# Mixture-of-experts layer on one core: run each expert whole on TensorE, and load the last weights in the order of their use

## The chip, the cores and the metric

One core of one Trainium2 chip runs the whole program. The metric is the device time of one execution in microseconds (us); lower is better. The kernel before takes 1175.49 us, the median of 3 runs (1172.38 to 1176.23).

## The reference, cut to what matters

A decoder layer on 256 tokens of width 1024, in float32: a mixer of three attention groups and a layer norm, then a mixture of 32 experts, of which each token takes 4, and a second layer norm. The change concerns the experts alone:

```
def expert_block(args):
    e, tok, w = args
    xb = xt[tok]
    gu = xb @ w_gu[e] + b_gu[e]
    gate = jnp.minimum(gu[:, :D_EXPERT], SWIGLU_LIMIT)
    up = jnp.clip(gu[:, D_EXPERT:], -SWIGLU_LIMIT, SWIGLU_LIMIT)
    act = gate * jax.nn.sigmoid(SWIGLU_ALPHA * gate) * (up + 1.0)
    y = act @ w_dn[e] + b_dn[e]
    return (y * w[:, None]).astype(h.dtype)
```

Each expert has 1024 x 2048 gate-up weights and 1024 x 1024 down weights, 8.39 MB and 4.19 MB, and all of them are read from HBM once: 403 MB.

## The kernel before, in words

Each engine has its own program, written out by hand, and semaphores between them. The mixer ends at about 180 us; then the router picks the experts, and the experts run, two to a loop pass (`PAIRS` = 16; the loop has 15 passes).

**Slots.** An expert works on 64 token slots; a gather (L1032) is a matmul of x with a 0/1 matrix and serves both experts of a pair, in two halves of the width, into PSUM banks 6 and 4. ScalarE (ACT) copies both to `xg` in SBUF. Where an expert has more than 64 tokens, blocks of 32 more slots run in `extra_blocks` (L1178), whose count is read from SBUF into a register of each engine (`value_load`, a TENSOR_LOAD in the trace).

**PE, per expert.** `gate_up` (L1074): 4 chunks of 16 instructions, and the bias; results in banks 4 and 5. VectorE (DVE) and ACT make the activation (L1621 to L1627, sigmoid at L696). `act_transposes` (L1109) turns it over, ACT copies it to `actT` (L700), `down` (L1098) multiplies in 4 chunks into bank 7, from where ACT and DVE copy it to `ysb` (L712, L1665). Once a pair, `combine` (L1039) adds both experts' rows to the four accumulators in banks 0 to 3, with the weights `CT` that `weight_transposes` made.

**The order on PE** (loop at L1216): gate-up of expert 2i+1, down of 2i, gather, transposes for 2i+1, extra blocks of 2i+1, gate-up of 2i+2, down of 2i+1, transposes for 2i+2 and of the weights, combine, extra blocks of 2i+2. So down of an expert stands behind the gate-up of the next one.

**The weights.** SBUF holds gate-up weights of two experts (`gu_slot`) and down weights of one (`dn_slot`). SyncE (SP) loads them in chunks of 2 MB and 1 MB (`load_gu`, L347, `load_dn`, L352), all in one queue and in a fixed order (loop at L400): gate-up of expert e+2 when gate-up of e (and its extra blocks) has read a chunk (`guc`, `xguc`), then down of e+1 when down of e has (`dn_used`, `xdnc`). While SP waits for one, nothing behind it is issued. Behind the loop the last down is loaded, and then the parameters of the second layer norm (L426).

Of the kernel before, what the change touches and what calls it, by code (L numbers as in the profile page):

```python
# [13 lines left out]
P = 128  # L14
TOKENS = 256
TB = TOKENS // P
# [4 lines left out]
N_EXPERTS = 32  # L21
TOP_K = 4
PAIRS = N_EXPERTS // 2
# [5 lines left out]
GU_CHUNKS = 4  # L29
DN_CHUNKS = 4  # L30
# [26 lines left out]
def hybrid_layer(nc, x, w_in, b_in, pos_k, pos_v, w1_k, w2_k, w1_v, w2_v, g_out, w_out, ln1_g, ln1_b,  # L57
                 router_w, router_b, w_gu, b_gu, w_dn, b_dn, ln2_g, ln2_b, out):
    with ExitStack() as ctx:
# [255 lines left out]
        def _(sp_):  # L315
# [84 lines left out]
            with sp.Fori(0, PAIRS - 1) as i:  # L400
                for par in range(2):

                    count_extra_blocks(2 * i + par)
                    for c in range(GU_CHUNKS):
                        xc = use_by_extra_blocks(c)
                        sp.wait_ge(s["guc"], i * (2 * GU_CHUNKS) + (par * GU_CHUNKS + c + 1))
                        sp.wait_ge(s["xguc"], xc)
                        load_gu(i + 1, par, c)
                    for c in range(DN_CHUNKS):
                        xc = use_by_extra_blocks(c)  # L410
                        sp.wait_ge(s["dn_used"], i * (2 * DN_CHUNKS) + (par * DN_CHUNKS + c + 1))
                        sp.wait_ge(s["xdnc"], xc)
                        load_dn(i + par, 1 - par, c)

            count_extra_blocks(N_EXPERTS - 2)
            for c in range(DN_CHUNKS):
                xc = use_by_extra_blocks(c)
                sp.wait_ge(s["dn_used"], (N_EXPERTS - 2) * DN_CHUNKS + c + 1)
                sp.wait_ge(s["xdnc"], xc)
                load_dn(PAIRS - 1, 1, c)  # L420
# [102 lines left out]
        def _(act):  # L523
# [201 lines left out]
            sigmoid(1)  # L725
# [3 lines left out]
                           ACT.Copy).then_inc(s["ysb_ok"], 1)  # L729
            act_columns(5, 1)  # L730
            combine_weights(1)
            act.wait_ge(s["nx_ok"], 1)
            extra_blocks(0)
            with act.Fori(0, PAIRS - 1) as i:
                sigmoid(2 * i + 2)
                expert_output(0, 2 * i + 1)
                slots_to_sbuf(0, 6, 2 * i + 3)
                slots_to_sbuf(1, 4, 2 * i + 4)
                act_columns(6, 2 * i + 2)
                extra_blocks(2 * i + 1)  # L740
                sigmoid(2 * i + 3)
                expert_output(1, 2 * i + 2)
                act_columns(5, 2 * i + 3)
                combine_weights(i + 2)
                extra_blocks(2 * i + 2)
            sigmoid(N_EXPERTS)
            expert_output(0, N_EXPERTS - 1)
            act_columns(6, N_EXPERTS)
# [5 lines left out]
        def _(pe):  # L754
# [277 lines left out]
            def gather(h, bank):  # L1032
# [733 lines left out]
```

## Time and profile before

| | |
|---|---|
| median of 3 runs | 1175.49 us |
| the profiled execution | 1174.48 us |
| its span | 1172.5 us |
| mean granted TensorE clock | 0.98 |
| PE busy | 1071.5 us (91%) |
| LDWEIGHTS (PEld) busy | 458.4 us (39%) |
| DVE, ACT, POOL busy | 25%, 12%, 2% |
| moved by DMA | 426.32 MB, mean 364 GB/s |
| loads of gate-up weights | 128 of 2048 KB, median 30.4 us from issue to landing |
| loads of down weights | 128 of 1024 KB, median 24.0 us from issue to landing |

The profiled execution's own time is 2 us longer than its span. The page cuts the span in 40 slices of 29.3 us; the windows of the trace do the same for any stretch. Lines of PE are mostly L758, the helper that all matmuls go through, so groups are told apart by their tiles and counts: a gate-up is x64 instructions on `WB,S` 128*64, a down x32 of them, a gather x32 on `S,X`, a combine x8 on 128*128 x 512, and an extra block's gate-up x64 on 128*32.

### The profile page before, as it was taken

How to read it: one execution, taken by the hardware profiler on the slowest of the kernel's cores; microseconds unless marked ns; L12 is line 12 of the kernel's file. 1: busy time of each engine (PE TensorE's matmuls, PEld its weight loads, DVE VectorE, ACT ScalarE, POOL GpSimd, SP SyncE). 2: the span in 40 equal slices, each digit the busy share in tenths (PEclk: the TensorE clock that was granted, in tenths of full speed). 3: DMA queues.
4: the chain of work that ended last, by engine and by line, in shares of the span. 5: the costliest groups of instructions: out<-in, count | busy, mean ns of one | idle time of the engine just before them, and what ended most of it. 6: DMA issues, size and time to landing. Idle time of an engine off the chain costs nothing.

```text
span 1172.5 us, 14722 instructions
## 1 busy us (share of the span) xinstructions
PE 1071.5 (91%) x5364; PEld 458.4 (39%) x5365; DVE 291.3 (25%) x770; ACT 146.0 (12%) x313; POOL 29.2 (2%) x54
## 2 busy tenths in 40 slices
PE   7999897888999999998989889999999999999983
PEld 6778544332334333323233323333344333333321
DVE  2354645121212212121212212122212212121114
ACT  2044501010011110000000100001011000000000
POOL 3000400000000000000000000000000000000000
PEclk9999998998999999999999989999999999999997
DMA  9623439764999999999999998999999999999993
GB/s 311 247 110 72 168 137 386 301 241 191 405 427 425 428 427 425 428 427 425 427 427 425 427 427 338 427 425 427 427 425 427 427 426 426 427 426 426 427 420 134
DMA packets 48980, 426.32 MB, mean 364 GB/s; under 512 B 5034, under 2 KB 8923, under 8 KB 16155
## 3 DMA queue, kind: packets, MB, share of 16 engines
q1 hardware_dynamic: 48378, 425.37, 87.8%
q10 hardware_dynamic: 576, 0.61, 0.2%
q8 instruction: 16, 0.26, 0.1%
q14 instruction: 10, 0.07, 0.0%
HBM read 424.91 MB, written 1.05 MB: 363 GB/s over the span
## 4 chain that ended last, share of the span: by engine, by line
PE 62%; DMA 28%; DVE 4%; SPq 3%; issue 2%; ACT 1%; DVEq 0%
PE PB L758 60%; DMA WB<-in_w_gate_up_dram 24%; DMA WB<-in_w_down_dram 3%; SPq L347 2%; ACT S L660 0%; DVE S L1519 0%; DMA X<-in_x_dram 0%; PE PB L1112 0%; DVE K L1502 0%; DVE S L1730 0%; PE PB L765 0%; DVE S L1485 0%; SPq L356 0%; DVE S L1621 0%; DVE S L1622 0%
## 5 line engine op out<-in xcount | busy, mean ns | idle before, releaser
L758 PE MATMUL PB<-WB,S 128*64 128x512 f32 (+5 forms) x3456 | 761.7, 593 | 50.7 <-DMA WB<-in_w_gate_up_dram 25.1
L758 PEld LDWEIGHTS PB<-WB,S 128*64 128x64 f32 (+2 forms) x3456 | 250.8, 139 | 540.5 <-issue 456.2
L1621 DVE TENSOR_SCALAR S<-PB 128x512 f32<-128x512 f32 (+1 forms) x34 | 35.9, 1056 | 652.1 <-PE PB L758 652.1
L758 PE MATMUL PB<-S 32*64 32x512 f32 (+5 forms) x464 | 108.1, 589 | 4.3 <-ACT S L692 1.4
L696 ACT ACTIVATE S<-S 128x512 f32<-128x512 f32 x32 | 20.2, 630 | 552.2 <-DVE S L1621 552.2
L758 PEld LDWEIGHTS PB<-S,X 128*128 128x128 f32 x512 | 61.2, 199 | 13.3 <-issue 12.2
L758 PE MATMUL PB<-S,X 128*128 128x128 f32 x512 | 64.3, 286 | 1.0 <-DVE S L1563 1.0
L758 PE MATMUL PB<-S,WB 128*128 128x256 f32 (+2 forms) x336 | 62.2, 385 | 0.4 <-ACT S L534 0.4
L758 PEld LDWEIGHTS PB<-S 32*64 32x64 f32 (+5 forms) x464 | 34.9, 149 | 65.5 <-issue 54.1
L758 PEld LDWEIGHTS PB<-S,WB 128*128 128x128 f32 (+1 forms) x336 | 48.3, 175 | 12.2 <-issue 2.1
L758 PE MATMUL PB<-WB 128*32 128x128 f32 (+8 forms) x276 | 46.1, 354 | 4.4 <-DVE WB L1450 2.8
L1665 DVE COPY S<-PB 64x512 f32<-64x512 f32 x32 | 21.8, 683 | 106.8 <-PE PB L758 106.8
L712 ACT ACTIVATE S<-PB 64x512 f32<-64x512 f32 x32 | 19.0, 594 | 176.2 <-PE PB L758 176.2
L1622 DVE TENSOR_SCALAR S<-PB 128x512 f32<-128x512 f32 (+1 forms) x34 | 36.1, 1062 | 0.1
L758 PEld LDWEIGHTS PB<-WB 128*64 128x64 f32 (+2 forms) x276 | 29.5, 152 | 16.5 <-issue 12.2
L512 POOL TENSOR_TENSOR K<-K 128x1 f32<-128x1 f32 x4 | 3.9, 982 | 993.1 <-DVE K L1515 993.1
L660 ACT ACTIVATE S<-PB 128x512 f32<-128x512 f32 x32 | 19.1, 597 | 45.9 <-PE PB L758 45.9
L1624 DVE SCALAR_TENSOR_TENSOR S<-S 128x512 f32<-128x512 f32 (+1 forms) x34 | 23.5, 692 | 1.2
L1627 DVE TENSOR_TENSOR S<-S 128x512 f32<-128x512 f32 (+1 forms) x34 | 23.5, 691 | 1.2
L1112 PE MATMUL PB<-K,S 128*128 128x128 f32 x128 | 20.2, 280 | 2.3 <-DVE S L1627 2.3
L577 ACT ACTIVATE WB<-WB 128x128 f32<-128x128 f32 (+1 forms) x40 | 17.7, 443 | 21.9 <-DVE WB L1377 21.9
L1112 PEld LDWEIGHTS PB<-K,S 128*128 128x128 f32 x128 | 14.2, 141 | 15.6 <-issue 13.0
(208 smaller groups left out, 345.1 us busy)
## 6 DMA issues: line engine op xcount, KB each, us to landing
WB<-in_w_gate_up_dram SPq DMA_DIRECT2D x128, 2048.0 KB, 30.4
WB<-in_w_down_dram SPq DMA_DIRECT2D x128, 1024.0 KB, 24.0
WB<-in_w_in_dram SPq DMA_DIRECT2D x3, 2048.0 KB, 15.4
WB<-in_w_in_dram SPq DMA_DIRECT2D x1, 2144.0 KB, 10.5
WB<-in_w_in_dram SPq DMA_DIRECT2D x2, 1024.0 KB, 10.9
WB<-in_w_out_dram SPq DMA_DIRECT2D x2, 1024.0 KB, 10.2
WB<-in_w_out_dram SPq DMA_DIRECT2D x1, 2048.0 KB, 7.8
WB<-in_w_in_dram SPq DMA_DIRECT2D x1, 1040.0 KB, 13.5
```

The lines of the kernel that those rows point to most:

```text
L347: sp.dma_start(gu_slot[par][:, kk * c:kk * c + kk, :], src[:, c // 2, 2 * (c % 2):2 * (c % 2) + 2, :]).then_inc(s_gul[par][c], 16)
L577: ins = act.activation(l[:, a:b], l[:, a:b], ACT.Exp, bias=nmx[u % 3][:, c:c + 1], accum_out=sm[u % 3][:, c:c + 1])
L660: act.activation(xg[:, 4 * h:4 * h + 4, :].rearrange("p k s -> p (k s)"), PB[bank][:, :], ACT.Copy)\
L696: act.activation(act_sb, gt, ACT.Sigmoid, scale=SWIGLU_ALPHA).then_inc(s["sig"], 1)
L712: act.activation(ysb[64 * e:64 * e + 64, 1, :], PB[7][64:128, :], ACT.Copy).then_inc(s["ysb_ok"], 1)
L758: return mm_(o, l, r, start=start, stop=stop, skip_group_check=True)
L1112: ins = tr(PB[bank][:, P * c:P * c + P], act_sb[:, P * c:P * c + P], ident)
L1621: ts(by_rows(g), in_order(gate), LIMIT, None, ALU.min).then_inc(s[g_ok], 1)
L1622: ts(by_rows(u), in_order(up), LIMIT, -LIMIT, ALU.min, ALU.max).then_inc(s[clip], 1)
L1624: stt(u, u, 1.0, g, ALU.add, ALU.mult).then_inc(s[upg], 1)
L1627: tt(a, u, a, ALU.mult).then_inc(s[done], 1)
L1665: cp(ysb[64 * e:64 * e + 64, 0, :], PB[7][0:64, :]).then_inc(s["ysb_dv"], 1)
```

## The change

On PE an expert now runs whole: gate-up, three quarters of the gather (for the odd experts) or of the combine (for the even ones, for the pair before), transposes, the last quarter, extra blocks, down. All transposes go to bank 5. ACT and DVE copy the outputs of an expert behind its extra blocks, and ACT copies the transposed activation between the two halves of the gather. For the first expert, ACT makes `CT` before the sigmoid and the combine stands ahead of the transposes. An extra block waits for the copies of banks 4 and 6 ahead of its own gather. On SP the loop is a pass shorter; the last pass is written out with the down loads ahead of the gate-up loads.

```
-            with sp.Fori(0, PAIRS - 1) as i:
+            def next_gu(i, par):
+                for c in range(GU_CHUNKS):
+                    xc = use_by_extra_blocks(c)
+                    sp.wait_ge(s["guc"], i * (2 * GU_CHUNKS) + (par * GU_CHUNKS + c + 1))
+                    sp.wait_ge(s["xguc"], xc)
+                    load_gu(i + 1, par, c)
+
+            def next_dn(i, par):
+                for c in range(DN_CHUNKS):
+                    xc = use_by_extra_blocks(c)
+                    sp.wait_ge(s["dn_used"], i * (2 * DN_CHUNKS) + (par * DN_CHUNKS + c + 1))
+                    sp.wait_ge(s["xdnc"], xc)
+                    load_dn(i + par, 1 - par, c)
+
+            with sp.Fori(0, PAIRS - 2) as i:
                 for par in range(2):
                     count_extra_blocks(2 * i + par)
...
+                    next_gu(i, par)
+                    next_dn(i, par)
+
+            for par in range(2):
+                count_extra_blocks(N_EXPERTS - 4 + par)
+                next_dn(PAIRS - 2, par)
+                next_gu(PAIRS - 2, par)
             count_extra_blocks(N_EXPERTS - 2)
...
+            next_dn(PAIRS - 1, 0)
```

ACT (the loop; DVE's copies of the outputs move likewise):

```
             with act.Fori(0, PAIRS - 1) as i:
                 sigmoid(2 * i + 2)
-                expert_output(0, 2 * i + 1)
                 slots_to_sbuf(0, 6, 2 * i + 3)
+                act_columns(5, 2 * i + 2)
                 slots_to_sbuf(1, 4, 2 * i + 4)
-                act_columns(6, 2 * i + 2)
                 extra_blocks(2 * i + 1)
+                expert_output(1, 2 * i + 2)
                 sigmoid(2 * i + 3)
-                expert_output(1, 2 * i + 2)
                 act_columns(5, 2 * i + 3)
                 combine_weights(i + 2)
                 extra_blocks(2 * i + 2)
+                expert_output(0, 2 * i + 3)
```

PE:

```
-            def extra_blocks(e, loaded, t, pb6_copied, copies, outputs_copied):
+            def extra_blocks(e, loaded, t, pb4_pb6_copied, copies, outputs_copied):
...
                     with pe.Fori(0, count):
+                        pe.wait_ge(s[pb4_pb6_copied], copies)
                         extra_gather()
-                        pe.wait_ge(s[pb6_copied], copies)
...
-            act_transposes(5, 1)
-            weight_transposes()
             pe.wait_ge(s["ysb_ok"], 1)
             pe.wait_ge(s["bdn_ld"], 16)
             combine()
+            act_transposes(1)
+            weight_transposes()
             extra_blocks(0, 1, 0, "ct_sb", 1, 0)
+            down(0, 1, 1, first=True)
             with pe.Fori(0, PAIRS - 1) as i:
-                pe.wait_ge(s["actT"], 2 * i + 1)
                 gate_up(1, i + 1, 2 * i + 2)
-                down(0, i + 1, 2 * i + 1)
                 pe.wait_ge(s["ohs"], i + 2)
                 pe.wait_ge(s["ct_sb"], i + 1)
                 gather(0, 6)
                 pe.wait_ge(s["g_ok"], 2 * i + 2)
-                gather(1, 4)
-                pe.wait_ge(s["xg_ok"], 2 * i + 3)
-                act_transposes(6, 2 * i + 2)
+                gather(1, 4, range(2))
+                act_transposes(2 * i + 2)
+                gather(1, 4, range(2, 4))
+                extra_blocks(1, i + 1, 2 * i + 1, "xg_ok", 2 * i + 4, 2 * i + 1)
+                down(1, i + 1, 2 * i + 2)
+
                 pe.wait_ge(s["xg_ok"], 2 * i + 4)
-                extra_blocks(1, i + 1, 2 * i + 1, "actT", 2 * i + 2, 2 * i + 1)
-
                 gate_up(0, i + 2, 2 * i + 3)
-                down(1, i + 1, 2 * i + 2)
-                act_transposes(5, 2 * i + 3)
-                weight_transposes()
                 pe.wait_ge(s["ysb_ok"], 2 * i + 3)
                 pe.wait_ge(s["ysb_dv"], 2 * i + 2)
-                combine()
+                combine(range(3))
+                act_transposes(2 * i + 3)
+                weight_transposes()
+                combine(range(3, 4))
                 extra_blocks(0, i + 2, 2 * i + 2, "ct_sb", i + 2, 2 * i + 2)
+                down(0, i + 2, 2 * i + 3)
```

What stands in a row on PE in the first half of the loop (an odd expert): `WB,S` x32 is a gate-up, x16 a down, `S,X` x16 a gather. Before:

```order
L758 MATMUL PB<-WB,S 64x512 x32
L1079 REGISTER_ALU
L758 MATMUL PB<-S 64x512 x4
L758 MATMUL PB<-WB,S 64x512 x16
L1221 REGISTER_ALU
L758 MATMUL PB<-S,X 128x128 x16
L1226 REGISTER_ALU
L1112 MATMUL PB<-K,S 128x128 x4
L1228 REGISTER_ALU
L1180 ISA
L1180 TENSOR_LOAD nx
```

And of the change, where L766 is the helper of all matmuls and L1123 the transposes:

```order
L766 MATMUL PB<-WB,S 64x512 x32
L1089 ISA
L766 MATMUL PB<-S 64x512 x4
L1232 REGISTER_ALU
L766 MATMUL PB<-S,X 128x128 x12
L1123 MATMUL PB<-K,S 128x128 x4
L766 MATMUL PB<-S,X 128x128 x4
L1191 ISA
L1191 TENSOR_LOAD nx
```

The down between bias and gather is gone; it stands behind the extra block now, and the load of the block count (`nx`) follows the last quarter of the gather. Before, the ISA row ahead of that load holds a wait for the second copy of the gathered rows (`xg_ok`); in the change it holds none.

The first expert on PE, behind its bias, where the row of `S 128x512 x4` is the combine. Before:

```order
L1112 MATMUL PB<-K,S 128x128 x4
L1117 MATMUL PB<-K,S 128x128 x2
L758 MATMUL PB<-S 128x512 x4
L1180 TENSOR_LOAD nx
L1180 ISA x2
```

And of the change:

```order
L766 MATMUL PB<-S 128x512 x4
L1123 MATMUL PB<-K,S 128x128 x4
L1128 MATMUL PB<-K,S 128x128 x2
L1191 TENSOR_LOAD nx
L1191 ISA x2
```

The combine moved ahead of the transposes, and the first down (not shown) stands between the extra block and the loop's entry, no longer behind the gate-up of the loop's first pass.

## Rows read from the trace of the kernel before

**Rows 1.** The page: GB/s in 40 slices of 29.3 us; the chain by engine

```profile
GB/s 311 247 110 72 168 137 386 301 241 191 405 427 425 428 427 425 428 427 425 427 427 425 427 427 338 427 425 427 427 425 427 427 426 426 427 426 426 427 420 134
...
PE 62%; DMA 28%; DVE 4%; SPq 3%; issue 2%; ACT 1%; DVEq 0%
```

**Rows 2.** Windows: us, busy (x count) of PE, PEld, DVE, ACT, POOL, PEclk, DMA share, GB/s

```profile
225.00:226.00 1.00, 1.00 (x8) 0.43 (x6) 0.00 (x0) 0.00 (x0) 0.00 (x0) 1.00 0.50 197
...
225.00:245.00 20.00, 20.00 (x98) 6.57 (x96) 5.29 (x16) 0.63 (x1) 0.00 (x0) 1.00 0.18 60
250.00:260.00 10.00, 7.81 (x78) 2.61 (x82) 0.00 (x0) 1.30 (x4) 0.00 (x0) 1.00 0.68 265
275.00:295.00 20.00, 20.00 (x98) 6.35 (x96) 3.67 (x6) 0.63 (x1) 0.00 (x0) 1.00 0.18 57
705.00:720.00 15.00, 14.93 (x70) 5.20 (x67) 6.12 (x17) 1.82 (x3) 0.00 (x0) 1.00 0.67 247
```

**Rows 3.** Timeline of one pair, PE and DVE: start us, us, engine, line, operation, count

```profile
716.75 0.66 PE L1112 MATMUL PB<-K,S 128*128 128x128 f32 x4
...
717.70 3.67 PE L758 MATMUL PB<-S 128*128 128x512 f32 x8
...
721.30 13.95 PE L758 MATMUL PB<-WB,S 128*64 128x512 f32 x64
...
736.20 7.09 PE L758 MATMUL PB<-WB,S 128*64 128x512 f32 x32
...
739.06 0.69 DVE L1627 TENSOR_TENSOR S<-S 128x512 f32<-128x512 f32 x1
...
743.22 3.84 PE L758 MATMUL PB<-S,X 128*128 128x128 f32 x32
```

**Rows 4.** The chain in that pair: start us, us, what

```profile
747.70 1.14 issue
```

**Rows 5.** Timeline of experts 0 and 1, PE and SP's queue

```profile
215.89 0.66 PE L1112 MATMUL PB<-K,S 128*128 128x128 f32 x4 [2.30 <-DVE S L1627]
...
216.62 5.28 PE L758 MATMUL PB<-S 128*128 128x512 f32 x8
...
223.65 13.95 PE L758 MATMUL PB<-WB,S 128*64 128x512 f32 x64 [1.75 <-issue]
...
238.55 7.09 PE L758 MATMUL PB<-WB,S 128*64 128x512 f32 x32
...
241.19 5.05 SPq L352 DMA_DIRECT2D WB<-in_w_down_dram  x4
...
251.22 1.07 PE L758 MATMUL PB<-X,S 128*32 128x256 f32 x16 [1.38 <-issue]
...
253.70 7.07 PE L758 MATMUL PB<-WB,S 128*32 128x512 f32 x64 [0.47 <-ACT S L675]
...
255.84 5.46 SPq L347 DMA_DIRECT2D WB<-in_w_gate_up_dram  x4
...
273.57 1.99 PE L758 MATMUL PB<-S 64*128 64x512 f32 x8 [0.71 <-ACT S L692]
```

**Rows 6.** In expert 1's extra block: a PE row of the timeline, and a window

```profile
265.51 0.69 PE L1164 MATMUL PB<-K,S 128*128 128x128 f32 x2 [3.74 <-DVE S L1627]
...
267.00:270.00 3.00, 2.67 (x16) 0.83 (x20) 0.00 (x0) 0.23 (x1) 0.00 (x0) 0.50 1.01 431
```

**Rows 7.** Timeline of PE at the end

```profile
1099.17 3.65 PE L758 MATMUL PB<-WB,S 128*64 128x512 f32 x16 [1.25 <-DMA WB<-in_w_gate_up_dram]
...
1141.39 0.66 PE L1112 MATMUL PB<-K,S 128*128 128x128 f32 x4
...
1142.77 3.65 PE L758 MATMUL PB<-WB,S 128*64 128x512 f32 x16 [0.73 <-ACT S L700]
...
1149.96 1.94 PE L758 MATMUL PB<-WB,S 128*64 128x512 f32 x8 [0.56 <-DMA WB<-in_w_down_dram]
...
1152.77 3.67 PE L758 MATMUL PB<-S 128*128 128x512 f32 x8 [0.88 <-DVE S L1665]
```

More of the change, by code:

```diff
@@ L729, in _ @@
                            ACT.Copy).then_inc(s["ysb_ok"], 1)
+            sigmoid(1)
             act_columns(5, 1)
@@ L733, in _ @@
             extra_blocks(0)
+            expert_output(0, 1)
             with act.Fori(0, PAIRS - 1) as i:
                 sigmoid(2 * i + 2)
-                expert_output(0, 2 * i + 1)
                 slots_to_sbuf(0, 6, 2 * i + 3)
+                act_columns(5, 2 * i + 2)
                 slots_to_sbuf(1, 4, 2 * i + 4)
-                act_columns(6, 2 * i + 2)
                 extra_blocks(2 * i + 1)
+                expert_output(1, 2 * i + 2)
                 sigmoid(2 * i + 3)
-                expert_output(1, 2 * i + 2)
                 act_columns(5, 2 * i + 3)
@@ L745, in _ @@
                 extra_blocks(2 * i + 2)
+                expert_output(0, 2 * i + 3)
             sigmoid(N_EXPERTS)
-            expert_output(0, N_EXPERTS - 1)
-            act_columns(6, N_EXPERTS)
+            act_columns(5, N_EXPERTS)
             extra_blocks(N_EXPERTS - 1)
@@ L1030, in _, with gather @@
             acc = lambda b, h: PB[2 * b + h]
-            def gather(h, bank):
-                for k in range(4):
+            def gather(h, bank, parts=range(4)):
+                for k in parts:
                     for b in range(TB):
@@ L1036, in gather, with combine @@
                                  oh[:, b, :], k == 0 and b == 0, b == TB - 1)
-                ins.then_inc(s["ga"], 1)
-            def combine():
-                for b in range(TB):
-                    for h in range(2):
-                        ins = mm(acc(b, h)[:, :], CT[:, b, :], ysb[:, h, :], False, False)
-                ins.then_inc(s["comb"], 1)
+                if k == 3:
+                    ins.then_inc(s["ga"], 1)
+            def combine(parts=range(4)):
+                for n in parts:
+                    b, h = n // 2, n % 2
+                    ins = mm(acc(b, h)[:, :], CT[:, b, :], ysb[:, h, :], False, False)
+                if n == 3:
+                    ins.then_inc(s["comb"], 1)
             def gate_up_chunk(c, e):
@@ L1107, in down, with act_transposes @@
                     down_chunk(c).then_inc(s["dn_used"], 1)
-            def act_transposes(bank, n):
+            def act_transposes(n):
                 pe.wait_ge(s["act"], n)
                 for c in range(4):
-                    ins = tr(PB[bank][:, P * c:P * c + P], act_sb[:, P * c:P * c + P], ident)
+                    ins = tr(PB[5][:, P * c:P * c + P], act_sb[:, P * c:P * c + P], ident)
                 ins.then_inc(s["at"], 1)
@@ L1707, in _ @@
             next_one_hots(0)
+            expert_output(0, 1)
             with dve.Fori(0, PAIRS - 1) as i:
@@ L1711, in _ @@
                 first_extra_slots(2 * i + 1)
-                expert_output(0, 2 * i + 1)
                 extra_blocks(2 * i + 1, 2 * i + 2)
+                expert_output(1, 2 * i + 2)
                 expert_activations(2 * i + 3)
@@ L1716, in _ @@
                 first_extra_slots(2 * i + 2)
-                expert_output(1, 2 * i + 2)
                 extra_blocks(2 * i + 2, 2 * i + 3)
                 next_one_hots(i + 1)
+                expert_output(0, 2 * i + 3)
             expert_activations(N_EXPERTS)
             first_extra_slots(N_EXPERTS - 1)
-            expert_output(0, N_EXPERTS - 1)
             extra_blocks(N_EXPERTS - 1, N_EXPERTS)
```

22 lines of the change are left out of this document (2 added, 20 removed).

## The prediction, made before the changed kernel ran

> **What bounds the kernel now.** I read the page's slices first [rows 1]. From 293 us on the DMA engines move 425 to 428 GB/s in nearly every slice, so the queue of expert weights is at its full rate; but the chain of waits is PE for 62% and DMA for 28%. Both are near their limit, and a saving on one alone is not a saving of the kernel. So I look at where each waits for the other.
>
> The queue runs dry in four places [rows 2]. At 426 GB/s, 225:245 loses 20 x (1 - 60/426) = 17.2 us, 250:260 loses 3.8, 275:295 loses 17.3, and 705:720 loses 6.3 us: 44.6 us, all while PE is nearly full. Where it is not short, the 25.17 MB of a pair of experts take 59.1 us at its 426 GB/s. PE alone needs less [rows 3]: gate-up with bias 736.20 - 721.30 = 14.90 us, down 743.22 - 736.20 = 7.02, gather with transposes and wait 5.62 (743.22 to 748.84, the end of the row in [rows 4]), and for the other expert 14.90 + 7.02 + 0.95 (transposes, 716.75 to 717.70) + 3.60 (combine). That is 54.0 us a pair. In the 5.62 us is a bubble of 1.14 us [rows 4]: the sequencer waits for the second copy to SBUF and only then reads the number of extra blocks.
>
> Why the queue runs dry is in the order at the first experts [rows 5]. The down weights of expert 1 go where those of expert 0 are, and down of expert 0 stands behind gate-up of expert 1: it starts at 238.55, SP issues at 241.19, while the bytes of the loads before it were through at about 225.6 (225:226 moved 197 GB/s, the last microsecond with much in it [rows 2]). Expert 1 has an extra block (from 251 to 275.5), so its gate-up slot is free only from 255.84, and its down comes after gate-up of expert 2, at about 290. Expert 15 has one too, and repeats the last part at 705.
>
> **The change part by part.** No matmul, byte or DMA is added; all is moved.
>
> *First expert.* Down of expert 0 now follows combine and transposes. Combine no longer waits for the activation: it can start where PE's gap of 2.30 us begins, at 215.89 - 2.30 = 213.6, takes at most 5.3 us, transposes 0.95: down at about 219.8. Its first chunk is free at 221.7, ahead of 225.6. The first dry stretch goes: 17.2 us back.
>
> *Second dry stretch.* Now it opens earlier, at 225.6 + 9.8 = 235.4 us, since the 4.19 MB of down weights are already in. Gate-up of expert 1 starts at 219.8 + 7.0 = 226.8, 3.2 later than before. Its extra block starts at 226.8 + 14.9 + 5.0 (below) + 0.7 (copy) = 247.4, its first weight chunk is read from 249.9 (251.22 to 253.70 was 2.5), and SP issues 2.1 later [rows 5], and I put 1.4 until bytes flow (250:260 lost 3.8, of which the rest is this start): 253.4. This costs 18.0 where 3.8 were lost.
>
> *Third.* Those loads end at 253.4 + 19.7 = 273.1. The extra block ends 21.8 us after 249.9 (253.70 to 275.5 before), at 271.7, and down of expert 1 follows at once, not after another gate-up. SP issues 2.6 us after a down starts and the smaller chunks flow some 2.4 later (what 225:245 moved, 2.8 us of it, leaves room for 1.4 at its end): 276.7, so 3.6 instead of 17.3 (and 0.6 of ramp). *Fourth*, by the same steps at expert 15: about 3 instead of 6.3. Sum before 45.2, now 24.6: **20.6 us more of moving data**.
>
> *The loop.* Between bias and transposes stands the activation, 739.75 - 736.20 = 3.55 us [rows 3]. Three quarters of a gather (2.8) or combine (2.7) cover most of it; 0.8 us of PE are idle. Then transposes 0.50 and a quarter gather 0.95, or transposes 0.95 and a quarter combine 0.90. The copy of the transposed activation (0.6) ends within that. An expert costs 14.90 + 5.0 + 7.02 = 26.9 or 27.3 us: 54.2 a pair against 54.0. DVE and ACT do the same in another order; their copies of the outputs have 20 us until they are needed. The value load now has no wait of its own ahead of it, only matmuls that carry theirs. Two rows bound it: 1.14 us where its own wait precedes it [rows 4], none where a combine does (717.70 to 721.30 is the combine alone, [rows 3]). I take 0, since matmuls stand ahead of it as in the second row, and keep both for the range. The Trainium skill ("TensorE: Matmul & The Clock Gate", the spec table) gives TensorE's queue 64 entries; by that the sequencer passes all of gather and transposes and reads early. The trace agrees only for the combine.
>
> *The last loads.* With expert-whole order, the last gate-up would stand in the queue ahead of a down that PE wants first. Swapping them for experts 28 and 29 makes the queue's end dn 28, dn 29, gu 30, dn 30, gu 31, dn 31, in order of use. SP's wait for gate-up now stands behind one for down; down of 28 is consumed chunk by chunk as it lands, so nothing runs dry. The loads of ln2's parameters stay behind, over before they are wanted.
>
> *The end.* In the old order the last byte landed at 1149.96 and only a quarter of a down, combine and layer norm followed [rows 7]. Now more stands behind the data. Last tie of PE to the queue: down of 28. Before, gate-up 30 landed at 1099.17, so dn 28, ahead of it, at 1099.2 - 19.7 = 1079.5; now 20.6 earlier, 1058.9. Its last chunk (1.9) ends at 1060.8; PE alone could be there at 278.7 (end of down 1) + 27 x 27.1 + 24.3 (expert 15's extra) = 1034.7, so 26 us of slack, and the data decide. Expert 29: 26.9, expert 30: 27.3, to 1115.0 (its own data are in). Expert 31: 14.9 + 3.55 + 1.38 (1141.39 to 1142.77, transposes and copy) + 7.02 + 0.87 + 3.7 (copy and combine, 1151.9 to 1156.46) = 31.4: 1146.4.
>
> *The clock.* After gate-up of 31 nothing covers the 3.55 us. After a gap of 3.74 us in an extra block the granted clock stood at 0.50, the 1.2 GHz level, for the matmuls that followed [rows 6]. About 4 us at half rate cost 2 (0 if it stays up, 3 if the whole down is slow). End of combine at **1148.4**, against 1156.46: 8.1 us earlier. The Trainium skill (same page, "Part 1: The HAM clock gate") says that the slow level is the default and activity lifts it; by that, the new last gap costs, and this speaks against the change. The trace agrees at the gap named.
>
> The layer norm behind it does not change. Profiled execution 1174.48 - 8.1 = **1166.4 us**. That execution was 1.0 below the median of the runs shown (1175.49), within their spread.
>
> **The rivals.**
> *A, the value load stays bare (slower).* If PE reads the number only when it gets to it, 1.14 us are added to each expert, and some 0.2 where quarter and transposes no longer cover the copy: 1.34. PE is then the bound: 1034.7 + 54.2 + 31.4 + 30 x 1.34 + 2 (clock) = 1162.5, 6 us after 1156.46: 1180.5. It decides from 0.96 us an expert (26/27) and turns into a loss from 1.14 (34/30). For it: the bubble [rows 4], and 1.75 at the loop's entry [rows 5] behind 5 us of combine. Against: the combine rows. 0.12.
> *B, no change.* The data come earlier, but half of it is lost: the first dry stretch stays in part (if combine waits for its weights or the loop entry costs its 1.75 and starves the queue), or the half clock spreads over the end. 8 to 10 us later than forecast: about 1175. 0.11.
> *C, more gain.* Expert 15's stretch goes wholly, the clock holds, and PE needs 0.3 less an expert: 3 + 2 + 1: about 1160. 0.12.
> *D, the swap starves the queue.* Dn 29 can be asked for only as down of 28 reads its chunks while they land; a chunk's turn is 1.9 (read) + 0.3 + 2.4 (until bytes flow) = 4.6 us, under the 7.4 that three chunks in flight last. If the turn is not covered, the queue and all behind it lose 4.6: 1171. 0.05.
> Forecast: 0.60.
>
> **How the numbers follow.** The forecast's own range is 1162 to 1170 (clock 0 to 3, dry stretches +-2). Down to C and up to B it is 1160 to 1176, which leaves out A and edges of C, below 2 in 10. 0.3% is 3.5 us, about what a measurement of this kernel can tell: faster than 1172 are forecast, C and D, with part of B: 0.79; within: 0.11; slower: A without its lightest cases, 0.10.
>
> **What would show it.** In the new trace: 225:235 at full rate and one long dry stretch at 235:253; the next under 5 us; pairs of 54 us while PE is behind, 59 while data are; no gap between the quarter and down; last byte about 18 us ahead of the last combine, not 3; half clock after the gap at 1130. Wrong if PE's experts take over 28 us, if dn 1 is issued after 225, or if the queue is dry at other places.

## The result, and the profile after

The changed kernel takes 1178.71 us (median of 16 runs, 1175.09 to 1181.92) against 1175.08 for the kernel before on the same chips (16 runs, 1172.38 to 1178.03). The ratio is 1.0035, 95% interval 1.0025 to 1.0045: **0.35% slower**, where 8.1 us (0.7%) less were forecast. The profiled execution took 1177.09 us (span 1174.9).

The page, GB/s in 40 slices of 29.4 us and the chain by engine, against [rows 1]:

```profile
GB/s 310 269 88 72 184 153 399 343 90 377 426 427 426 427 426 426 427 426 427 426 426 426 426 351 423 426 426 427 426 427 426 427 427 428 424 427 424 426 337 36
...
PE 59%; DMA 29%; DVE 9%; issue 2%; SPq 1%; ACT 1%; DVEq 0%
```

Once the experts run, the queue is short only around the first ones and around expert 15. Its loss in a slice is 29.4 x (1 - GB/s / 426). Over slices 8 to 37 that was 44.2 us before and is 37.2 now: 7.0 us gained where 20.6 were forecast. At the end the last full slice is the 38th; the 39th has 337 where it had 420, the 40th 36 where it had 134: the last byte comes earlier, and more work stands behind it. The chain has 9% of DVE where it had 4%: it runs through an activation wherever PE waits for its end.

Windows of the first experts and of expert 15, against [rows 2] (same columns):

```profile
222.00:226.00 4.00, 4.00 (x10) 1.28 (x12) 0.00 (x0) 0.00 (x0) 0.00 (x0) 0.50 0.34 139
...
220.00:240.00 20.00, 18.06 (x72) 6.35 (x74) 0.68 (x1) 0.59 (x1) 0.00 (x0) 0.83 0.73 280
...
235.00:240.00 5.00, 5.00 (x26) 1.83 (x24) 0.00 (x0) 0.00 (x0) 0.00 (x0) 1.00 0.79 321
...
240.00:265.00 25.00, 21.13 (x146) 8.91 (x145) 6.17 (x19) 3.19 (x6) 0.00 (x0) 0.86 0.15 53
...
257.00:259.00 2.00, 2.00 (x12) 0.39 (x8) 0.00 (x0) 0.00 (x0) 0.00 (x0) 0.50 0.00 0
...
280.00:290.00 10.00, 10.00 (x50) 3.30 (x48) 0.68 (x1) 0.59 (x1) 0.00 (x0) 1.00 0.80 277
675.00:685.00 10.00, 8.74 (x86) 2.75 (x90) 0.22 (x2) 0.77 (x2) 0.00 (x0) 1.00 0.82 318
...
677.00:680.00 3.00, 2.53 (x26) 0.79 (x29) 0.00 (x0) 0.38 (x1) 0.00 (x0) 1.00 0.62 257
...
700.00:710.00 10.00, 10.00 (x50) 3.35 (x48) 0.68 (x1) 0.59 (x1) 0.00 (x0) 1.00 0.81 290
```

220:240 loses 6.9 us, of which 1.2 in 235:240 already belong to the next stretch: 5.6 are left of the first (forecast: 0). The second is 1.2 + 21.9 in 240:265 (18.0), the third 3.5 in 280:290 (3.6), the fourth 2.5 + 3.2 in 675:685 and 700:710 (about 3). In 220:240 and 240:265 the granted clock is 0.83 and 0.86, with 0.50, the 1.2 GHz level, at 222:226 and 257:259. Before, it was 1.00 in each window of [rows 2].

The timeline of PE at experts 0 and 1, against [rows 5]:

```profile
195.63 13.95 PE L766 MATMUL PB<-WB,S 128*64 128x512 f32 x64 [0.69 <-ACT S L668]
...
215.50 0.38 PE L1128 MATMUL PB<-K,S 128*128 128x128 f32 x2
221.94 23.67 PE L766 MATMUL PB<-WB,S 128*64 128x512 f32 x96 [6.06 <-issue]
245.55 1.09 PE L766 MATMUL PB<-S 32*64 32x512 f32 x8
...
250.66 1.06 PE L766 MATMUL PB<-S,X 128*128 128x128 f32 x8
253.95 1.07 PE L766 MATMUL PB<-X,S 128*32 128x256 f32 x16 [2.23 <-DVE S L1658]
...
256.69 9.62 PE L766 MATMUL PB<-WB,S 128*32 128x512 f32 x64 [0.47 <-ACT S L683]
...
280.42 20.82 PE L766 MATMUL PB<-WB,S 128*64 128x512 f32 x96
```

and SP's queue there:

```profile
226.30 6.17 SPq L352 DMA_DIRECT2D WB<-in_w_down_dram  x4
260.54 6.30 SPq L347 DMA_DIRECT2D WB<-in_w_gate_up_dram  x4
```

The rows of x96 are a down (x32) and the next gate-up (x64). The transposes of expert 0 are over at 215.9, but its down starts at 221.94: 6.06 us in which PE waits for nothing that the profile shows. The chain of waits has the copy of the transposed activation, 0.6 us, and then

```profile
216.31 5.63 issue
```

The same 96 instructions take 20.82 us at 280.42 and 23.67 here. Then the gather of the extra block waits 2.23 us for DVE's one-hots (before, 1.38 of "issue" alone), and its gate-up takes 9.62 us where it took 7.07 [rows 5]. So SP issues the next gate-up loads at 260.54 (before, 255.84).

PE in the steady part and at the end, against [rows 3] and [rows 7]:

```profile
306.48 1.02 PE L766 MATMUL PB<-S 128*128 128x512 f32 x2
...
360.35 1.02 PE L766 MATMUL PB<-S 128*128 128x512 f32 x2
...
494.93 1.06 PE L766 MATMUL PB<-S,X 128*128 128x128 f32 x8
496.37 1.94 PE L766 MATMUL PB<-WB,S 128*64 128x512 f32 x8 [0.38 <-DMA WB<-in_w_down_dram]
...
1069.41 15.67 PE L766 MATMUL PB<-WB,S 128*64 128x512 f32 x72 [0.56 <-DMA WB<-in_w_down_dram]
...
1138.88 1.09 PE L766 MATMUL PB<-S 32*64 32x512 f32 x8
1143.53 1.08 PE L1123 MATMUL PB<-K,S 128*128 128x128 f32 x4 [3.57 <-DVE S L1638]
1145.31 9.06 PE L766 MATMUL PB<-WB,S 128*64 128x512 f32 x32 [0.69 <-ACT S L708]
1155.25 3.67 PE L766 MATMUL PB<-S 128*128 128x512 f32 x8 [0.88 <-DVE S L1676]
```

A pair takes 53.9 us where PE sets the pace (306.48 to 360.35). Between the last quarter and the down there is only a wait for weights (494.93 to 496.37), none for the number of extra blocks. The last tie of PE to the queue is the last chunk of down 28, at 1069.41. From there nothing waits for data until the combine ends at 1158.92, 89.5 us later. Before, those were 1156.46 - 1079.5 = 77.0 us.

### The profile page after: what moved, and what is told of

Its sections match the earlier page's. It is cut to its first block, busy times and chain, and to the rows that moved or that the text cites. A ratio compares the mean times of both kernels' runs of the same rounds, so it can differ in the third digit from the quotient of the medians.

```text
span 1174.9 us, 14685 instructions
## 1 busy us (share of the span) xinstructions
PE 1070.8 (91%) x5364; PEld 461.1 (39%) x5365; DVE 290.6 (25%) x770; ACT 147.7 (13%) x313; POOL 29.2 (2%) x54
## 4 chain that ended last, share of the span: by engine, by line
PE 59%; DMA 29%; DVE 9%; issue 2%; SPq 1%; ACT 1%; DVEq 0%
PE PB L766 57%; DMA WB<-in_w_down_dram 28%; DVE S L1632 2%; DVE S L1633 2%; DVE S L1635 1%; DVE S L1638 1%; PE PB L1123 1%; DMA WB<-in_w_in_dram 1%; DVE S L1530 0%; DVE K L1513 0%; DVE S L1741 0%; DVE S L1496 0%; SPq L330 0%; DVE WB L1415 0%; DVE S L1658 0%
## 5 line engine op out<-in xcount | busy, mean ns | idle before, releaser
L766 PE MATMUL PB<-WB,S 128*64 128x512 f32 (+5 forms) x3456 | 758.4, 595 | 30.8 <-DMA WB<-in_w_down_dram 21.4
L766 PEld LDWEIGHTS PB<-WB,S 128*64 128x64 f32 (+2 forms) x3456 | 255.6, 140 | 513.6 <-issue 440.2
L766 PE MATMUL PB<-S 32*64 32x512 f32 (+5 forms) x464 | 108.1, 586 | 3.2 <-ACT S L700 1.4
L1676 DVE COPY S<-PB 64x512 f32<-64x512 f32 x32 | 21.9, 684 | 264.9 <-PE PB L766 264.9
L704 ACT ACTIVATE S<-S 128x512 f32<-128x512 f32 x32 | 20.2, 630 | 473.0 <-DVE S L1632 473.0
L766 PE MATMUL PB<-S,X 128*128 128x128 f32 x512 | 66.1, 284 | 1.0 <-DVE S L1574 1.0
L766 PEld LDWEIGHTS PB<-S,X 128*128 128x128 f32 x512 | 61.8, 198 | 13.3 <-issue 12.2
L766 PE MATMUL PB<-S,WB 128*128 128x256 f32 (+2 forms) x336 | 60.2, 377 | 1.0 <-ACT S L542 0.5
L766 PEld LDWEIGHTS PB<-S 32*64 32x64 f32 (+5 forms) x464 | 33.1, 147 | 65.2 <-issue 58.0
L766 PEld LDWEIGHTS PB<-S,WB 128*128 128x128 f32 (+1 forms) x336 | 46.5, 170 | 12.3 <-issue 2.1
L766 PE MATMUL PB<-WB 128*32 128x128 f32 (+8 forms) x276 | 45.9, 353 | 4.4 <-DVE WB L1461 2.8
L1123 PE MATMUL PB<-K,S 128*128 128x128 f32 x128 | 21.4, 290 | 24.6 <-DVE S L1638 24.6
L766 PEld LDWEIGHTS PB<-WB 128*64 128x64 f32 (+2 forms) x276 | 29.4, 152 | 16.4 <-issue 12.2
L1123 PEld LDWEIGHTS PB<-K,S 128*128 128x128 f32 x128 | 13.8, 143 | 41.2 <-DVE S L1638 36.3
L708 ACT ACTIVATE S<-PB 128x512 f32<-128x512 f32 x32 | 19.1, 597 | 66.0 <-PE PB L1123 66.0
L668 ACT ACTIVATE S<-PB 128x512 f32<-128x512 f32 x32 | 19.1, 597 | 15.2 <-PE PB L766 15.2
```

What stands on the lines that cost most here:

```text
L668: act.activation(xg[:, 4 * h:4 * h + 4, :].rearrange("p k s -> p (k s)"), PB[bank][:, :], ACT.Copy)\
L704: act.activation(act_sb, gt, ACT.Sigmoid, scale=SWIGLU_ALPHA).then_inc(s["sig"], 1)
L708: act.activation(actT[:, :, :].rearrange("p c s -> p (c s)"), PB[bank][:, :], ACT.Copy)\
L766: return mm_(o, l, r, start=start, stop=stop, skip_group_check=True)
L1123: ins = tr(PB[5][:, P * c:P * c + P], act_sb[:, P * c:P * c + P], ident)
L1676: cp(ysb[64 * e:64 * e + 64, 0, :], PB[7][0:64, :]).then_inc(s["ysb_dv"], 1)
```

## The experiments

The forecast had two halves: the queue moves 20.6 us more, and 12.5 us more of PE's work stands behind the last tie. The theory after the result: the second half is right, and the first was eaten at two places, the hold ahead of down 0 and the late one-hots of the extra block, each followed by slow matmuls. The rivals are that the loop itself is slower (the bare value load), that the swap of the last loads costs, or that the hold is the value load and not the test and jump behind it. The first one falls by the trace above: no pair shows a gap there.

All lines below come from the page and the timeline of the run named. "Lost" is the sum over slices 8 to 37 as above, "tie" the start of the last chunk of down 28 (for the kernel before, the 1079.5 of the prediction), "start" that of gate-up 0. The ratio is to the kernel before in the same round of runs, where its median was 1174.3 to 1175.4.

| kernel | median us | ratio [95%] | lost | tie | start |
|---|---|---|---|---|---|
| before | 1175.08 | 1 | 44.2 | 1079.5 | 197.4 |
| the change | 1178.71 | 1.0035 [1.0025, 1.0045] | 37.2 | 1069.4 | 195.6 |
| e1_nocheck | 1170.90 | 0.9964 [0.9951, 0.9976] | 31.5 | 1063.9 | 195.7 |
| e2_downfirst | 1169.81 | 0.9950 [0.9933, 0.9966] | 31.9 | 1064.3 | 196.0 |
| e9_value_read_only | 1171.33 | 0.9970 [0.9957, 0.9982] | 30.7 | 1065.9 | 197.6 |
| e3_early_onehots | 1171.17 | 0.9972 [0.9958, 0.9987] | 28.3 | 1063.1 | 197.7 |
| e10_before_early_onehots | 1174.60 | 0.9999 [0.9988, 1.0011] | 44.9 | | 197.6 |
| e4_old_loads | 1184.14 | 1.0078 [1.0063, 1.0094] | 34.2 | 1066.7 | 195.6 |
| e5_both | 1165.50 | 0.9921 [0.9907, 0.9935] | 23.2 | 1056.2 | 195.8 |
| e6_both_fills | 1160.90 | 0.9884 [0.9867, 0.9900] | 22.4 | 1054.9 | 195.5 |
| e7_after_noextra | 1143.62 | 0.9748 [0.9730, 0.9766] | 3.4 | 1036.2 | 195.2 |
| e8_before_noextra | 1145.39 | 0.9752 [0.9738, 0.9767] | 18.0 | | 195.8 |
| e11_noextra_downfirst | 1142.70 | 0.9731 [0.9712, 0.9751] | -0.2 | 1035.5 | 197.5 |
| e12_swap_three_pairs | 1155.64 | 0.9833 [0.9815, 0.9851] | 23.2 | | 197.3 |

How to read it: tie minus lost is 1032.2 to 1033.0 in every profile that starts its experts at 195.2 to 196.0, and 1034.8 to 1035.7 in those that start at 197.4 to 197.7. So the tie follows the lost time one for one, and a profile has one of two starts, about 2 us apart in the first gate-up, whatever the kernel. Single profiles compare to 2 or 3 us only: e4, whose code is that of the change up to the last loads, lost 34.2 us where the change lost 37.2, and its profiled execution is 4.1 us under its median. So times are taken from the medians. (e12 loads in another order, so that its tie isn't the same one.)

### The hold ahead of the first down: e1, e2, e9

e1 leaves out the block count's test of expert 0, which has no extra block:

```
-            extra_blocks(0, 1, 0, "ct_sb", 1, 0)
             down(0, 1, 1, first=True)
```

> The changed kernel without PE's check for extra blocks of expert 0, which has none (nothing of the result changes). Theory 1 (the new order starts the first down late because PE's sequencer is held by that check, and every microsecond of dry queue at the first experts is one of time): the gap of 5.6 us ahead of the first down shrinks to under 1.5, down 0 runs at the full clock (7.0 us, not 9.7), gate-up of expert 1 starts 7 to 8 us earlier after the start of gate-up 0, the queue's loss in 220:240 falls from 7 us to under 2, and the time falls by 6 to 8 us against the changed kernel (about 1171). If the hold-up is in the entry of the loop, the gap moves to gate-up 1 and 3 us or less are gained. Rival (the down waits for its weights or for the copied activation): the gap stays and the time is the changed kernel's. Rival (PE's pace sets the end, not the queue): the gap goes, the time does not.

e2 keeps it, behind the down (ACT and DVE copy the outputs of expert 0 ahead of their own test):

```
-            extra_blocks(0, 1, 0, "ct_sb", 1, 0)
             down(0, 1, 1, first=True)
+            extra_blocks(0, 1, 0, "ct_sb", 1, 1)
```

> The changed kernel with down of expert 0 ahead of its extra blocks. Theory 1: the sequencer's check now lies under the 7 us of the down, so down 0 starts about 0.7 us after the transposes' end and at the full clock; if the hold-up lasts no longer than the down, gate-up 1 follows without a gap and the time falls by 6 to 8 us as without the check; if it lasts longer, some 1 to 2 us of gap stand behind the down and 5 to 7 are gained. Rival (weights or activation late): down still at about 26 us after gate-up 0 starts, no gain.

e9 reads the number into the register and makes nothing of it:

```
-            extra_blocks(0, 1, 0, "ct_sb", 1, 0)
+            pe.value_load(nx[0:1, 0:1], min_val=0, max_val=MAX_EXTRA)
```

> The changed kernel where PE, for expert 0, still reads the number of extra blocks but has neither the comparison nor the block's code (expert 0 has no extra block). It tells apart what holds the sequencer. Theory a (the read of the value): the gap ahead of the first down stays at 5 to 6 us and so does the time. Theory b (the jump over the block's code, to code that the sequencer does not have yet): the gap falls to under 1.5 us, as without the check, and the time is within 1 us of that kernel's (1170.9).

The first down in the timelines, e1:

```profile
216.39 20.82 PE L766 MATMUL PB<-WB,S 128*64 128x512 f32 x96 [0.47 <-ACT S L708]
...
245.56 1.94 PE L766 MATMUL PB<-X,S 128*32 128x256 f32 x16 [2.24 <-DVE S L1657]
...
249.16 8.52 PE L766 MATMUL PB<-WB,S 128*32 128x512 f32 x64 [0.47 <-ACT S L683]
```

e2:

```profile
216.73 20.82 PE L766 MATMUL PB<-WB,S 128*64 128x512 f32 x96 [0.47 <-ACT S L708]
```

e9, which is one of the late starters:

```profile
218.30 20.82 PE L766 MATMUL PB<-WB,S 128*64 128x512 f32 x96 [0.47 <-ACT S L708]
```

All three agree: the gap is 0.47 us for ACT's copy, and down 0 with gate-up 1 takes 20.82 us instead of 23.67, so the slow matmuls there came from the gap. The medians are 7.8, 8.9 and 7.4 us under the change. The lost time is 5.3 to 6.5 us less than in the change's profile, but only 2.3 to 3.5 less than in that of e4; in the three, both extra blocks have the slow gate-up that is treated below, in the change and in e4 only one. All three are faster than the kernel before, by 0.3 to 0.5%.

e9 shows which part held PE. With the value load alone, the down starts with ACT's copy. So the read costs nothing that can be seen, and in the change's own trace the load of the number is over at 214.9, 7 us before the down starts. What held was the test of the number or the jump over the code of the extra block, which expert 0 takes before anything of that code has run; no run takes these two apart. In e2 the same test stands behind down 0, and its 7 us of queued matmuls stand ahead of it: no gap stands inside the x96.

The hold was in the old profile too. Its gate-up of expert 1 started at 223.65, with only 1.75 us of "issue" ahead of it [rows 5], because a combine of 5.28 us was running. e3 (below) starts its experts at the same time as the kernel before and has its first down at 223.57: PE goes on at the same moment, and only the cover has gone. That PE is held until then in both is read from these two starts; no run measures the hold under the combine. The Trainium skill ("Runtime: NRT & Kernel Launch", "Instruction fetch mechanics") says that a taken branch whose target is outside the window of fetched code forces a fetch before execution goes on. The 5.63 us that went with the test and the jump would fit that, but no view here shows a fetch, and not every first pass costs them. With no extra blocks (e7, below), PE first jumps over the block of expert 1 with a gap of 0.38 us:

```profile
249.66 0.65 PE L766 MATMUL PB<-WB,S 128*64 128x512 f32 x2 [0.38 <-issue]
```

So why this jump held PE, and that one hardly, stays open.

In e1 the gather of the extra block still waits 2.24 us for DVE, and its gate-up takes 8.52 us: the second place is another one.

### The late one-hots: e3, e10

DVE makes the one-hots of an extra block behind the expert's activation. e3 makes them ahead of it, for all experts alike:

```
+                first_extra_slots(2 * i + 1)
                 expert_activations(2 * i + 2)
                 next_expert_rows(0, 2 * i + 1)
-                first_extra_slots(2 * i + 1)
```

> The changed kernel with DVE making an expert's first one-hot matrices for an extra block ahead of the expert's activation, where it waits for PE anyway. Theory (in the new order they are on the path: PE's gather of the extra block waits 2.23 us for DVE L1658, twice, experts 1 and 15): that wait goes, the extra blocks start 1.5 to 2.2 us earlier, and the time falls by 2 to 3 us (the two dry stretches that they open shrink). Rival (the extra block is bound elsewhere, or its time is hidden): the wait goes and the time stays within 1 us.

```profile
223.57 22.57 PE L766 MATMUL PB<-WB,S 128*64 128x512 f32 x96 [5.57 <-issue]
...
253.08 1.07 PE L766 MATMUL PB<-X,S 128*32 128x256 f32 x16 [0.81 <-ACT S L668]
...
255.56 7.07 PE L766 MATMUL PB<-WB,S 128*32 128x512 f32 x64 [0.47 <-ACT S L683]
```

The wait is 0.81 us, for ACT, and the gate-up takes 7.07 us, at expert 15 too. The median is 7.5 us under the change, where I had expected 2 to 3. With 1.4 us of wait at each of the two experts goes the slow gate-up, 2.5 us, which stood at one of the two in the change's profile (9.62 and 7.07) and in that of e4 (7.07 and 9.37): some 5.3 us together. Where the rest comes from, no run shows. The first down is held as before, so this wait is another place than the hold.

e10 makes the same edit in the kernel before.

> The kernel before with DVE's one-hot matrices made ahead of the activation, as in the earlier experiment on the changed kernel. Theory (the wait for them is new with the change: before, a whole down and a gather stood between the activation and the extra block): nothing gained, within 1 us of before. Rival (the edit helps any order): 5 us or more faster, and its 7.5 us are no part of the change's loss.

It gains nothing (0.9999), and the gather of the extra block still waits 1.38 us of "issue", not for DVE. In the kernel before, a down and a whole gather stood between a gate-up and its transposes, so that activation and one-hots were long done. In the change only three quarters of a gather stand there, and the wait is new with it.

### Both places: e5

> The changed kernel with both edits: down of expert 0 ahead of its extra blocks, and DVE's one-hot matrices for an extra block ahead of the activation. Theory 1 (what is lost at the first experts is lost once and adds up: 5.6 us of gap with 2.7 of half clock, and per extra block 2.2 us of wait with up to 2.5 of half clock behind it): gate-up 1 starts 7 to 8 us earlier than in the changed kernel, both extra blocks' gate-ups run at the full clock (7.1 us), and the time falls by 12 to 15 us against the changed kernel: 1164 to 1167. Rival (both edits take away the same dry stretch): no better than either alone, 1169 to 1171.

```profile
GB/s 310 268 96 73 176 135 389 424 185 396 427 426 426 426 427 426 426 425 426 428 425 426 404 371 428 427 426 427 425 428 425 428 425 427 426 427 426 425 329 36
```

1165.50 us, 13.2 under the change and 0.8% faster than before. 23.2 us are lost: close to the 24.6 of my forecast, and the time is close to the 1166.4 that I had given for the change itself. The eighth slice is at 424. So the two places make up the miss in time. Part of that agreement is luck: slices 8 to 11, the first experts, lose 18.5 us where I had 21.6, and slices 20 to 26, expert 15, lose 5.0 where I had about 3. And the two edits don't quite add: alone they gain 8.9 and 7.5 us, 16.4 together, but 13.2 in e5. No run shows where the other 3 us go.

### The swap of the last loads: e4, e12

e4 has the last loads in the old order (the loop of SP to `PAIRS - 1` again).

> The changed kernel with the last loads in the old order (gate-up 30 ahead of down 29, gate-up 31 ahead of down 30). Theory (down 29 then gets its weights 19.7 us later, which uses up 10 us of slack and then 5 of time): down of expert 29 waits for data, the end is 4 to 6 us later (about 1183). Rival (the order of the last loads is idle): the same time as the changed kernel.

```profile
1066.65 15.67 PE L762 MATMUL PB<-WB,S 128*64 128x512 f32 x72 [0.54 <-DMA WB<-in_w_down_dram]
...
1096.16 15.67 PE L762 MATMUL PB<-WB,S 128*64 128x512 f32 x72 [0.55 <-DMA WB<-in_w_down_dram]
...
1125.67 15.67 PE L762 MATMUL PB<-WB,S 128*64 128x512 f32 x72 [0.54 <-DMA WB<-in_w_down_dram]
```

Two more downs wait for their last chunk, and the experts between take 29.5 us instead of 26.9 and 27.3. From the tie at 1066.65 the combine ends 95.2 us later, not 89.5; the median is 5.4 us above the change (expected: 4 to 6). So the swap earns about 5 us here, and the rival that it costs falls.

e12 starts the order of use three pairs before the end, on top of e6 (below):

```
-            with sp.Fori(0, PAIRS - 2) as i:
+            with sp.Fori(0, PAIRS - 4) as i:
...
+            for j in range(PAIRS - 4, PAIRS - 1):
+                for par in range(2):
+                    count_extra_blocks(2 * j + par)
+                    next_dn(j, par)
+                    next_gu(j, par)
```

> The kernel with both edits and the fillers, with the last loads in the order of use from three pairs before the end (experts 24 to 29), not one. Theory (PE is tied to the queue at down 28 and runs 87.5 us from there alone; an earlier swap puts down weights 19.7 us earlier at more experts, so that PE is tied earlier and may run ahead at 27 us an expert instead of 29.5): 3 to 7 us faster, 1154 to 1158. Rival (the swapped order asks for down weights only when a down is running, and the queue runs dry between): new dry spots between 940 and 1100 us, same or slower.

```profile
939.06 15.67 PE L767 MATMUL PB<-WB,S 128*64 128x512 f32 x72 [0.55 <-DMA WB<-in_w_down_dram]
...
1117.00 3.65 PE L767 MATMUL PB<-WB,S 128*64 128x512 f32 x16 [1.27 <-DMA WB<-in_w_gate_up_dram]
```

The last wait for down weights is now at 939. From there the queue's loads come in the order of use, PE draws level with them by and by, and it is the last gate-up's last chunk, at 1117.00, that it waits for last: behind that stands only expert 31's own activation, down and combine. 1155.64 us, 5.3 under e6 (expected: 3 to 7) and the best of all. No slice between 940 and 1100 us is under 424 GB/s, so the queue doesn't run dry there. That is 1.7% faster than the kernel before, 23 us under the change.

### The clock: e6

e6 adds 15 matmul calls on the identity, 30 instructions in the trace, where PE would be idle for an activation: ahead of the last transposes, and the like in the extra block. Their results are not used.

```
             gate_up(1, PAIRS, N_EXPERTS)
             pe.wait_ge(s["ct_sb"], PAIRS)
+            for n in range(15):
+                mm(PB[6][:, 0:P], ident, ident, True, True)
```

> The last one, with 30 matmul instructions of 128 columns into a free bank in each of PE's three long gaps (before the transposes of expert 31 and of the two extra blocks); they compute nothing that is used. Theory (a gap of 3.6 us drops the granted clock to the 1.2 GHz level, and the down behind it pays 2 us): the last down takes 7.1 us, not 9.1, the extra blocks' downs 3.6, not 5 to 6; the time falls by 3 to 5 us against the kernel without them (2 at the end, the rest from earlier data). Rival (the clock is set by something else, or the fillers delay the transposes): downs as long as before, same time or up to 1 us longer.

The end in e5:

```profile
1130.39 1.09 PE L1123 MATMUL PB<-K,S 128*128 128x128 f32 x4 [3.57 <-DVE S L1638]
1132.17 9.22 PE L766 MATMUL PB<-WB,S 128*64 128x512 f32 x32 [0.69 <-ACT S L708]
```

and in e6:

```profile
1125.36 3.62 PE L766 MATMUL PB<-K 128*128 128x128 f32 x30
1128.95 0.66 PE L1123 MATMUL PB<-K,S 128*128 128x128 f32 x4
1130.31 7.09 PE L766 MATMUL PB<-WB,S 128*64 128x512 f32 x32 [0.70 <-ACT S L708]
```

The last down takes 7.09 us instead of 9.22, the transposes 0.66 instead of 1.09. From the last bias to the end of the combine it is 17.6 us instead of 20.2: 2.6 us. The tie is 1.4 us earlier by the fills in the extra blocks, whose downs take 3.64 us where e5 has 5.01 and 6.00. Together 4.0, measured 4.6 between the medians (expected: 3 to 5).

It would be more, had the hold not come back. Slices 20 to 26 lose 0.5 us instead of 5.0, but slice 11 has 352 GB/s where it had 427, a new loss of 5.0 us. Ahead of down 2, where e5 has no gap, the chain has

```profile
293.01 5.47 issue
```

and the 96 matmuls behind it take 22.92 us instead of 20.82. Here, too, the load of the number was long over (at 292.0). This is the first time that PE passes this test in the loop, and it jumps over a block that is longer by the fills. e12 has the same gap, 5.89 us. Whether the longer code is the cause was not tested; the two runs show only that with the fillers the hold is back, at another place.

### Without extra blocks: e7, e8, e11

e7 (the change) and e8 (before) set all block counts to zero, so they leave out the tokens beyond 64 of experts 1 and 15:

```
-            link(ts(n_sum[0], count, float(SLOTS), None, ALU.is_gt))
+            link(ts(n_sum[0], count, float(SLOTS + 10000), None, ALU.is_gt))
```

> The changed kernel with the counts of extra blocks set to zero: the tokens beyond 64 of experts 1 and 15 are left out. It shows the new order without extra blocks. Theory 1 (the new order loses against my sum at the first down and in the two extra blocks): the queue is dry only around 222 to 230 and for some 3 us around 235 to 240, and the time is about 1150, some 29 us below the changed kernel. Rival (the loop itself is slower than summed): pairs take over 55 us where PE is behind.

> The kernel before with the counts of extra blocks set to zero, likewise. By the ledger of the queue only the first dry stretch (17.2 us) is left, so it falls by 27 us, to about 1148: the change is then at 0 to +2 us of it (forecast without the held-up first down: 6 us better). If the change is 5 us or more better here, its loss lies in the extra blocks alone and the held-up first down costs nothing.

The window in which e7 is short:

```profile
220.00:235.00 15.00, 14.11 (x60) 5.11 (x62) 0.68 (x1) 0.59 (x1) 0.00 (x0) 0.89 0.82 312
```

and that of e8:

```profile
220.00:250.00 30.00, 26.87 (x143) 11.32 (x144) 4.37 (x7) 3.29 (x6) 0.00 (x0) 1.00 0.42 157
```

Here the two accounts add up as in the forecast: one dry stretch of 18.0 us becomes 3.4, 14.6 gained, 12.5 given back behind the tie, 2.1 left. Measured between the medians: 1.8. My expectations for the two times were off: about 1150 for e7 (1143.62) and 1148 for e8 (1145.39), so the change came out faster here where I had put it level or slower. This is the ledger of the forecast without the extra blocks (the hold of the first down, 5.43 us, is still in it), and it shows how thin the margin is: with most of the dry time saved, the reordering alone is worth 2 us.

e11 is e7 with the down ahead of the test, as in e2.

> The changed kernel without extra blocks (counts zero, tokens beyond 64 of experts 1 and 15 left out) and with the first down ahead of the check. Theory (ledger of the queue: the end is the queue's data plus a fixed run of PE behind them): the queue loses under 0.5 us instead of 4.2 at 220:235, and the time falls by 4 us to 1139 to 1140, 5 to 6 under the kernel before without extra blocks: what my sum gave for the first dry stretch less the longer end. Rival (PE's pace sets the end here): the first down starts 5 us earlier and the end does not move.

```profile
205.00:240.00 35.00, 34.53 (x168) 12.15 (x164) 5.88 (x15) 3.75 (x6) 0.00 (x0) 1.00 1.01 426
```

The queue never runs dry, as expected, and PE still waits for weights at down 28, so that its own pace doesn't set the end. But the median is 0.9 us under e7's, not 4. This profile started its experts at 197.5 and e7's at 195.2, and the tie moved by 0.7 us for 3.6 us less lost; the two starts explain that pair of profiles. Whether they also explain the medians is open: the intervals of the ratios, 0.9712 to 0.9751 and 0.9730 to 0.9766, overlap, and no run records the start of an execution that was not profiled.

## Why the prediction was wrong

Point by point, by its own steps:

- **What bounds the kernel.** This was right. Both ties held: PE's pace until the queue sets it, and the last tie at down 28.
- **First expert.** This is the step that failed first. I sent down 0 off at 219.8, behind combine and transposes. These were over sooner than I had it (215.9), but the down started at 221.94, behind the test of the block count. A profile that starts its experts as late as the kernel before has that down at 223.57 (e3), so like for like it is 3.8 us late. The value load's price, taken as 0, was right; the test and jump behind it I had not priced at all. The row was there, "1.75 issue" at the loop's entry [rows 5], and I took it, in rivals A and B, for the whole price. It was the uncovered end of a hold that ran beneath a combine of 5.28 us. I moved that combine away. The stretch that "goes" kept 5.6 us. The matmuls after the gap, 23.67 for 20.82 us, put the next steps off by another 2.9.
- **Second dry stretch.** It lost 23.1 us for 18.0, and SP's issue came at 260.54 where my steps give 252.0. Some 5 of these 8.5 us come from the late and slow down 0. The rest is the chain behind gate-up 1, which took the one-hots as ready (0.7 for a copy; it was 2.23 for DVE) and the clock as full (7.07 for the extra block's gate-up; it was 9.62). DVE does the same work in the same order; PE comes to it sooner, with three quarters of a gather where a down and a gather were.
- **Third and fourth.** They lost 3.5 us for 3.6, and 5.7 for about 3. The one-hots came late at expert 15 too (2.19 us at 675), but they aren't the whole of it: e5, without that wait, still loses 5.0 us in slices 20 to 26, and e6, with the gap of 3.74 us inside the extra block filled, 0.5. What else made 5.7 of about 3 wasn't traced further.
- **The loop.** A pair took 53.9 us against 54.2, with no bubble at the value load. Rival A falls.
- **The last loads.** No wait came in at down 29. e4 prices the swap at 5.4 us; rival D falls.
- **The end.** From the tie 89.5 us, as worked out (1058.9 to 1148.4). The half clock behind the last gap cost 9.06 - 7.09 = 2.0 and 0.4 in the transposes; 2 was forecast.
- **The sum.** The tie came at 1069.41, not 1058.9: 10.5 us, nearly the whole miss of the profiled execution (1177.09 for 1166.4). Of the 10.1 us by which it moved at all, 7.0 are the queue's, and the rest goes with the earlier start of that execution. Against that stand 12.5 us of longer tail. By the two profiles that is 2.5 us slower, by the queue alone 5.5; the medians, over both kinds of start, differ by 3.6.

The nearest rival was B, by its mechanism (the first dry stretch stays in part, the loop entry starves the queue), but it had 8 to 10 us and a chance of 0.11, and its sum ended at no change. Rival A's 1180.5 is nearer to the measured time, but by luck: its bubble in each expert didn't come. That a gain of 20.6 is set against a certain loss of 12.5 should have made the range wider on the slow side: a miss of two fifths of the gain was enough to turn the sign. And my rival on the slow side was looked for in the loop, 30 times a small price, not in the one place where the gain was made.

## What to carry to other kernels

Keep two accounts for a kernel between a load queue and an engine: the time that the queue is dry, and the work that stands behind its last byte; a reorder that saves the first often adds to the second, for certain, while the saving hangs on a few places. When work is moved forward, ask of each row marked "issue" and of each helper engine's small work what was covering it: a branch over code that has not run yet may cost 5 to 6 us the first time (the change, e6) or next to nothing (e7), so look at its first pass in the trace and put it behind a long queued block (as in e2), the one-hots ahead of what delays them (e3). And a gap that has to stay is paid twice, by itself and in slower matmuls behind it; idle matmuls in it can buy the second part back (e6), if what they add to the code costs nothing elsewhere.

## What the runs showed of the hardware that was not expected

- The first jump over a block's code left PE idle for 5.4 to 6.1 us ahead of down 0 (the change, e3, e4, e7), while a register read alone in that place cost nothing that can be seen (e9). In the loop of the change no test leaves a gap. But in e6 and e12, whose block holds 30 more matmuls, the first pass of the test of expert 2 leaves 5.47 and 5.89 us, and the first jump over expert 1's block in e7 leaves 0.38.
- Short gaps were enough to bring the granted clock to 0.50 for part of the matmuls that followed. The extra block's gate-up takes 7.07 us at a clock of 1.00. Behind a gap of 2.2 us ahead of the block's gather (and the waits of 0.5 us that each of these blocks has) it took 8.52 to 9.72 in eight cases and 7.07 in two (the change, e4, e1, e2, e9; two experts each). With a gap of 0.81 it took 7.07 in each of eight cases (e3, e5, e6, e12). In the kernel before, a gap of 1.38 us at expert 1 left it at 7.07, and one of 1.34 at expert 15 did not:

```profile
671.21 8.41 PE L758 MATMUL PB<-WB,S 128*32 128x512 f32 x64 [0.47 <-ACT S L675]
```

- A gap of 3.57 us ahead of the last transposes cost 1.5 to 2.5 us in the down behind it, in each profile of the new order; with 30 small matmuls in it, none (e6, e12).
- The profiles fall into two kinds at the start, about 2 us apart by the first expert, with the kernels mixed over both. The second slice of the page tells them: 266 to 276 GB/s in the early ones, 238 to 247 in the late.
